# Weight split of a hybrid decoder layer: the gain moves from GpSimd into the ScalarE and VectorE splits, and the causal term of the first head from TensorE to VectorE

## What is computed

```python
def mixer_layer(x, conv_buf, c0, n0, m0, lead, norm_gain, w_in, ...):
    xn = rmsnorm(x, norm_gain)                       # x * rsqrt(mean x^2) * norm_gain
    proj = jnp.einsum('btd,dp->btp', xn, w_in)       # 1024 -> 9 * 512 + 8
    gb, gc, hc, zc, q, k, v, o, zm, ig, fg = jnp.split(proj, ...)
    yc, conv_new = short_conv(gc * hc, conv_buf, conv_w)
    y_conv = gb * yc * jax.nn.silu(zc)
    ...
    h = mlstm(q, k * HEAD_DIM ** -0.5, v, ig + b_igate, log_sigmoid(fg + b_fgate), state)
    ...                                              # per chunk of 128: exp(log_d - m), causal
    y_m = (rmsnorm(h) * mh_norm_gain * sigmoid(o)) * silu(zm)
    out = jnp.einsum('btw,wd->btd', concat([y_conv, y_m]), w_out)
    return x + out, ...
```

## Time and profile before

| | us |
|---|---|
| median of three runs | 1137.95 |
| lowest and highest run | 1137.59, 1143.83 |
| the profiled execution | 1141.33 |
| its span in the profile | 1139.5 |
| busy in the span: TensorE | 1071.2 (94%) |
| VectorE | 521.9 (46%) |
| ScalarE | 340.3 (30%) |
| GpSimd | 325.0 (29%) |
| mean granted TensorE clock | 0.985 |

### The profile page before, as it was taken

The page is one execution under the profiler, slowest core; times in us unless marked ns, Lnnn a source line. Parts: engine busy times, 40 slices in busy tenths (PEclk is TensorE's granted clock), DMA queues, the critical chain, the costliest instruction groups (busy, mean ns, idle before and its releaser), DMA issues. The chain is left out here.

```text
span 1139.5 us, 17968 instructions
## 1 busy us (share of the span) xinstructions
PE 1071.2 (94%) x7186; PEld 605.3 (53%) x7186; DVE 521.9 (46%) x981; ACT 340.3 (30%) x672; POOL 325.0 (29%) x370
## 2 busy tenths in 40 slices
PE   2799999998999999879999998899999999999996
PEld 2555546464666555536665655465656565444442
DVE  4886664555453434354433434544333233344333
ACT  6455534242412242322222223332222222221111
POOL 6432403043212323342122223431121111442322
PEclk9899999999999999999999999999999999999998
DMA  9464522043200311442002215310212044255652
GB/s 231 147 138 100 140 71 58 13 121 97 68 20 18 93 43 56 135 115 68 20 18 70 65 56 153 93 32 23 82 47 80 28 140 166 78 191 217 232 208 87
DMA packets 124184, 108.73 MB, mean 95 GB/s; under 512 B 42385, under 2 KB 109093, under 8 KB 124101
## 3 DMA queue, kind: packets, MB, share of 16 engines
q1 hardware_dynamic: 84160, 66.78, 20.1%
q0 software_dynamic: 7600, 25.03, 6.0%
q10 hardware_dynamic: 32340, 15.78, 5.2%
HBM read 65.43 MB, written 33.41 MB: 87 GB/s over the span
## 5 line engine op out<-in xcount | busy, mean ns | idle before, releaser
L824 PE MATMUL bank<-xTh,Wh 128*128 128x512 f16 (+2 forms) x1304 | 423.4, 344 | 7.9 <-DVE u L163 4.1
L825 PE MATMUL bank<-xTl,Wh 128*128 128x512 f16 (+2 forms) x1304 | 425.9, 344 | 0.0
L826 PE MATMUL bank<-xTh,Wl 128*128 128x512 f16 (+2 forms) x1304 | 425.0, 343 | 0.0
L826 PEld LDWEIGHTS bank<-xTh,Wl 128*128 128x128 f16 x1304 | 129.6, 99 | 122.0 <-issue 3.6
L824 PEld LDWEIGHTS bank<-xTh,Wh 128*128 128x128 f16 x1304 | 129.5, 99 | 117.9 <-DVE u L163 5.0
L825 PEld LDWEIGHTS bank<-xTl,Wh 128*128 128x128 f16 x1304 | 129.6, 99 | 109.8 <-issue 4.5
L833 PE MATMUL bank<-Wh,xTh 128*128 128x128 f16 x544 | 92.8, 219 | 1.4 <-DVE ysum L163 1.4
L835 PE MATMUL bank<-Wh,xTl 128*128 128x128 f16 x544 | 92.8, 219 | 0.0
L834 PE MATMUL bank<-Wl,xTh 128*128 128x128 f16 x544 | 92.8, 219 | 0.0
L610 POOL TENSOR_TENSOR wst<-wst,par 128x1024 f32<-128x1024 f32 x36 | 72.1, 2016 | 42.6 <-DMA wst<-in_w_in 42.3
L163 DVE SCALAR_TENSOR_TENSOR Wl<-wst,Wh 128x1024 f16<-128x1024 f32 x36 | 48.1, 1336 | 58.5 <-ACT Wh L163 56.3
(11 more groups left out here) (340 smaller groups left out, 1553.3 us busy)
## 6 DMA issues: line engine op xcount, KB each, us to landing
wst<-in_w_in ACTq DMA_DIRECT2D x27, 512.0 KB, 3.8
xs<-in_x_prompt SPq DMA_DIRECT2D x22, 512.0 KB, 4.0
y_ops<-ysumst POOLq DMA_DIRECT2D x16, 512.0 KB, 3.2
w_ops<-xs SPq DMA_DIRECT2D x16, 448.0 KB, 3.8
out<-xs POOLq DMA_DIRECT2D x11, 512.0 KB, 2.9
Wh<-y_ops SPq DMA_DIRECT2D x12, 448.0 KB, 3.6
Wl<-y_ops SPq DMA_DIRECT2D x12, 448.0 KB, 4.3
wst<-in_w_in SPq DMA_DIRECT2D x9, 512.0 KB, 4.9
```

The costliest lines, as they stand in the source:

```text
L824: mm(out, wh[:, k, :], xh, start=(k == 0), stop=False)
L825: mm(out, wh[:, k, :], xl, start=False, stop=False)
L826: last = mm(out, wl[:, k, :], xh, start=False, stop=(k == KT - 1))
```

## The change

GpSimd no longer multiplies weights by the gain. A new tile `wgain` holds 64 times the gain, and both splits take it as a scale for each partition. As the gain differs for each of the eight 128-row pieces k of a tile, each split is now eight instructions over 128 columns instead of one over 1024; each waits for the one before, and the other engine waits for the last. ScalarE's split waits for the load itself. In group 0 the two extra matmuls go, and the arguments are handled as in the other groups. The gate matmuls, the scan and the turn of blocks (0, 1) and (0, 2) come earlier. In the prologue the input parts of unit 3 come ahead of the gates' logits.

```diff
-GATES_AT = [ZC, HC, HC]
-SCAN_AT = [O, ZC, ZC]
-TURN_AT = [ZM, O, O]
+GATES_AT = [ZC, GC, GC]
+SCAN_AT = [O, GB, GB]
+TURN_AT = [ZM, ZC, ZC]
...
+        wgain = sb("wgain", [P, KT])
...
-            def gain_w(g, t):
-
-                pool.wait_ge(w_in_s[t % STAGES], g * (16 * NT // STAGES) + 16 * (t // STAGES + 1))
-                w = wst[t % STAGES]
-                pool.tensor_tensor(w[:, :, :], w[:, :, :], gain.unsqueeze(2).broadcast_to([P, KT, P]), ALU.mult).then_inc(w_gained, 1)
...
-                    if g:
-                        mm(A[:, :], selneg[:, :], m, start=True, stop=True).then_inc(a_full, 1)
-                    else:
-                        mm(A[:, :], selneg[:, :], m, start=True, stop=False)
-                        mm(A[:, :], identb[:, :], maskb[:, :].unsqueeze(1).broadcast_to([P, CH, P]), start=False, stop=True)\
-                            .then_inc(a_full, 1)
-                        pe.wait_ge(n_free, n)
-                        mm(N[0][:, :], selneg[:, :], m, start=True, stop=True).then_inc(e_full, 1)
+                    mm(A[:, :], selneg[:, :], m, start=True, stop=True).then_inc(a_full, 1)
...
-                act.wait_ge(w_gained, g * NT + (t + 1))
-                mark(fn(Wh[:, t, :, :], wst[t % STAGES][:, :, :], ACT.Copy, scale=WS).then_inc(w_high, 1), w_high, g * NT + (t + 1))
+                act.wait_ge(w_in_s[t % STAGES], g * (16 * NT // STAGES) + 16 * (t // STAGES + 1))
+                act.wait_ge(t1_free, 1)
+                for k in range(KT):
+                    last = fn(Wh[:, t, k, :], wst[t % STAGES][:, k, :], ACT.Copy, scale=wgain[:, k:k + 1])
+                    if k < KT - 1:
+                        did(last)
+                mark(last.then_inc(w_high, 1), w_high, g * NT + (t + 1))
...
             x_high_part(2)
             x_square(3)
+            x_high_part(3)
+            x_square(4)
             act.wait_ge(bias_in, 16 * 3)
             gate_logits(0, MIX, 1)
-            x_high_part(3)
-            x_square(4)
+            x_high_part(4)
             mixed_start(0, 0, K, True)
-            x_high_part(4)
...
                 dve.wait_ge(w_high, g * NT + (t + 1))
-                mark(stt(Wl[:, t, :, :], wst[t % STAGES][:, :, :], WS, Wh[:, t, :, :], ALU.mult, ALU.subtract).then_inc(w_low, 1), w_low, g * NT + (t + 1))
+                for k in range(KT):
+                    last = stt(Wl[:, t, k, :], wst[t % STAGES][:, k, :], wgain[:, k:k + 1], Wh[:, t, k, :], ALU.mult, ALU.subtract)
+                    if k < KT - 1:
+                        did(last)
+                mark(last.then_inc(w_low, 1), w_low, g * NT + (t + 1))
...
-                    if g:
-                        dve.wait_ge(a_full, n * 3 + 1)
-                        dve.wait_ge(y_sums, 4 * n)
-                        mark(tt(chunks(dp[:, :]), chunks(A[:, :]), maskb[:, :].unsqueeze(1).broadcast_to([P, CH, P]), ALU.add)
-                             .then_inc(arg_ready, 1), arg_ready, n + 1 - NB)
-                        dve.wait_ge(a_free, n * 3 + 1)
-                    else:
-                        dve.wait_ge(e_ready, n + 1)
+                    dve.wait_ge(a_full, n * 3 + 1)
+                    dve.wait_ge(y_sums, 4 * n)
+                    mark(tt(chunks(dp[:, :]), chunks(A[:, :]), maskb[:, :].unsqueeze(1).broadcast_to([P, CH, P]), ALU.add)
+                         .then_inc(arg_ready, 1), arg_ready, n + 1)
+                    dve.wait_ge(a_free, n * 3 + 1)
                     mark(tt(eh[:, :], eh[:, :], qf[:, :], ALU.mult).then_inc(q_scaled, 1), q_scaled, n + 1)
```

More of the change, by code:

```diff
@@ L295, in build @@
         xt_in = [sem(f"xt_in{i}") for i in range(3)]
-        w_gained, g_gained = sem("w_gained"), sem("g_gained")
+        g_gained, parts_clear = sem("g_gained"), sem("parts_clear")
         w_in_s = [sem(f"w_in{i}") for i in range(STAGES)]
@@ L304, in build @@
         a_full, a_free, s_full, s_free = sem("a_full"), sem("a_free"), sem("s_full"), sem("s_free")
-        e_full, e_ready, n_full, n_free = sem("e_full"), sem("e_ready"), sem("n_full"), sem("n_free")
+        n_full, n_free = sem("n_full"), sem("n_free")
         arg_ready, dp_ready = sem("arg_ready"), sem("dp_ready")
@@ L631, in _ @@
             x_power(4)
-            gain_w(0, 1)
-            gain_w(0, 2)
-            step(pool.memset(mparts[:, :], 0.0))
+            pool.memset(mparts[:, :], 0.0).then_inc(parts_clear, 1)
+            pool.wait_ge(parts_clear, 1)
             step(pool.memset(maskb[:, :], 0.0))
@@ L707, in store_mixed, with pool_block @@
                 pool.dma_start(dst, ystm[:, part, :, :]).then_inc(out, 16)
[L709 to L712, removed]
+            def pool_block(g, b, first):
                 for unit in ((), (11, 12), (15, 16))[b] if first else ():
                     x_power(unit)
-                weights(K, V)
                 if not (first and b == 0):
@@ L756, in _ @@
             for b in range(NB - 1):
-                pool_block(0, b, True, None)
+                pool_block(0, b, True)
             for g in range(1, H):
-                pool_block(g - 1, NB - 1, False, "weights")
+                pool_block(g - 1, NB - 1, False)
                 for b in range(NB - 1):
-                    pool_block(g, b, False, None)
-            pool_block(H - 1, NB - 1, False, None)
+                    pool_block(g, b, False)
+            pool_block(H - 1, NB - 1, False)
             store_y(H - 1, NB - 1, 1)
@@ L1253, in at_end @@
                     act.wait_ge(sel_ready, n + 1)
-                    if g:
-                        act.wait_ge(arg_ready, n + 1 - NB)
-                    else:
-                        act.wait_ge(ym_low, n)
-                        act.wait_ge(y_sums, 4 * n)
-                        act.wait_ge(a_full, n * 3 + 1)
-                    for out, src, kind, free, value in ((eh, A, 4, a_free, n * 3 + 1), (dp, dp, 3, dp_ready, n + 1 - NB)) if g else (
-                            (dp, A, 3, a_free, n * 3 + 1), (eh, N[0], 4, e_ready, n + 1)):
-                        if src is N[0]:
-                            act.wait_ge(e_full, n + 1)
+                    act.wait_ge(arg_ready, n + 1)
+                    for out, src, kind, free, value in ((eh, A, 4, a_free, n * 3 + 1), (dp, dp, 3, dp_ready, n + 1)):
                         for c in range(CH):
@@ L1649, in select @@
                 dve.wait_ge(tile_done, n * NT + 1)
-                if n <= NB:
-                    dve.wait_ge(e_ready, n)
-                else:
-                    dve.wait_ge(dp_ready, n - NB)
+                dve.wait_ge(dp_ready, n)
                 if b == 0:
@@ L1738, in at_end @@
                     if t == V:
+                        if b == 0:
+                            dve.wait_ge(parts_clear, 1)
                         gate_parts(tok0(b))
@@ L1818, in _ @@
             dve.wait_ge(t1_full, 1)
+            did(ts(wgain[:, :], T1[:, 0:KT], WS, None, ALU.mult))
             mark(copy(par[:, STATES_OUT:], T1[:, 0:PARAMS]).then_inc(t1_free, 1), t1_free, 1)
@@ L1826, in _ @@
             x_low_part(2)
+            x_low_part(3)
             dve.wait_ge(rows_const, 1)
```

17 lines of the change are left out of this document (1 added, 16 removed).

## The result

| | before | after |
|---|---|---|
| median of four runs, us | 1139.63 | 1178.97 |
| lowest and highest | 1137.59, 1143.83 | 1178.42, 1179.52 |
| span in the profile | 1139.5 | 1176.9 |
| busy: TensorE, VectorE, ScalarE, GpSimd | 1071.2, 521.9, 340.3, 325.0 | 1083.9, 563.1, 418.2, 246.1 |

The ratio is 1.034, with a 95% interval of 1.0307 to 1.0374: slower, where slower had been given 0.80. The time lies one us above the range. +25 us were predicted; the medians are 39.3 us apart, the two profiled executions and their spans 37.4.

What follows compares the result with a forecast made beforehand. TensorE, 94% busy, was taken to bound the kernel, with VectorE the engine making it wait. Terms 7.6 + 12 + 9.6 - 4.0 = +25 us gave 1163 us on the median; own range 1150 to 1174, whole range 1143 to 1178.

Steps and rivals of the forecast that it cites:

- The prices of a piece: Eight-piece splits: ScalarE piece 0.401 us, split 3.4 instead of 1.057; VectorE piece 0.349, split 3.05 instead of 1.23.
- Blocks (1,3) and (2,3): Same chain from a later load, new lateness partly replacing existing waits: 6 us each, together +12.
- Block (0,3): Step-by-step walk through both engines: the chunk waiting for update 0 comes 7.8 later; block loses 7.6 us.
- Block (0,0): Gates' rows 2.2 us earlier, mixed scores' product 8.9 later, then 2.9 more to the last state update: +9.6.
- The exponentials start about 2.0 later: Block (0,0), before the mixed scores' product: VectorE's mask addition stands behind a split and an input part, about 2.0 us.
- less about 3.1 of such waits: Block (0,0), last stretch: VectorE waits used up offset about 3.1 of O's 1.8 and ZM's 4.2, leaving +2.9.
- Blocks (0,1), (0,2): Scan moved -3.3, gate matmuls' wait in (0,1) +1.1, fewer matmuls in all four blocks -1.8: -4.0.
- the scan moves out: Scan leaves ZC in (0,1), ending TensorE's 1.67 us wait for the state, and one in the next block: -3.3.
- relief wins: First rival: GpSimd's relief outweighs splits if their pair in series takes 3.9 us, break-even 4.8; middle 1125 us, 8%.
- Late loads: Rival: ScalarE takes over GpSimd's load waits, showing at GB's split in three blocks, 3 x 3.7; 1174 us, 13%.
- Splits in between: Rival: pieces at 0.37 and 0.30, a pair of 5.3 us; 1144 us, 12%.
- no effect: Rival: splits cost nothing because they are off TensorE's path; 1132 us, 3%.

Runs made afterwards that it cites:

- e4: Changed kernel with pieces issued without waits between them and VectorE starting each piece when ScalarE's same piece is done; 1122.75 us, ratio 0.9841.
- e8: Changed kernel with no waits between pieces on either engine, VectorE still waiting for all eight of ScalarE's; 1138.81 us, ratio 0.9992.
- e5: Kernel before with only the first head's arguments changed: VectorE adds the mask, exponentials as in the other heads; 1143.51 us, ratio 1.0028.
- e6: Kernel before with only the three tables changed (places of gate matmuls, scan and turn); 1140.18 us, ratio 0.9997.
- e13: Changed kernel with throwaway matmuls filling TensorE's longest waits in blocks (0,3), (1,3), (2,3); 1179.67 us, ratio 1.0343.
- e1: Kernel before with only the eight-piece splits carrying the gain and GpSimd's multiplications gone; 1172.26 us, ratio 1.0274.
- e3: Changed kernel with both splits one 1024-column instruction with constant 64 and no multiplication by the gain anywhere; 1107.53 us, ratio 0.9709.
- e9: Changed kernel, waits between pieces kept, but VectorE starts each piece when ScalarE's same piece is done; 1162.84 us, ratio 1.0174.
- e11: Changed kernel with ScalarE's split one instruction with constant 64, VectorE's still eight pieces with the gain; 1151.44 us, ratio 1.0073.
- e15: Changed kernel with only ScalarE's eight pieces issued without waits between them; 1162.88 us, ratio 1.0196.
- e2: Changed kernel with GpSimd's gain and the long one-instruction splits kept, so only the rest of the change; 1144.42 us, ratio 1.0042.

## Why the prediction was right in kind and short in size

- **The prices of a piece** held: 0.401 on ScalarE, and 3.44 and 3.06 us a split. VectorE's form in PSUM was a good stand-in for SBUF. By the Trainium skill, "VectorE: DVE Perf Modes", section "The TRN2 errata", a split had been estimated at 2.3 and 1.6 us; without waits between pieces the rows show 2.44 and 2.19. The table is near ScalarE's independent instructions here, a quarter too low for VectorE's, and too low for chained ones on both. That the sum by the table would come near the first rival (1125) was not borne out: e4 (1122.75) is near it, but it also overlaps the engines; e8, without waits and in series as that rival has it, took 1138.81.
- **Blocks (1,3) and (2,3)**: +12 predicted, +13.1 measured. The walk through both engines' programs held for (1,3), and so did the argument that lateness replaces waits that were there. That the number fits so well is partly luck: (2,3) had been taken over from (1,3), and e5 and e6, which change nothing in these blocks, have (1,3) 2.4 and 1.7 and (2,3) 0.3 and 1.6 us shorter than the profile before, so each is known to about 2 us.
- **Block (0,3)**: +7.6 predicted, +11.4 measured. In the walk VectorE's split of V ends at 252.2. Counted from K's end (236.50 before, 249.33 after) it ended 1.1 us later: half is the steps between instructions, half GpSimd's additions beside it (3.60 instead of 3.06). `gcs` came 1.45 late, update 0 2.3 late, the last chunk 0.4 more, and a wait of 0.8 for `kfm` (the samples' keys, the first copy of the next block) stands behind ZM's split, where nothing had been counted. Small terms, all of one sign, are the error. The "two or three us" kept in hand for the clock were not it (e13). The walk had rightly put the exponentials behind the mask's addition and this behind the split of V: they start 18.5 us behind K's end, 17.2 in the walk, and 14.1 in e1, where TensorE adds the mask. This fits the 11.4 us that the block loses with both parts of the change, against 6.6 and 0.2 with each alone; a run of the splits with the arguments only was not made.
- **Block (0,0)**: +9.6 predicted, +12.55 measured. TensorE's start behind its waits for `drl`, `dpm` and `ysum`, before, after and in e1, cuts it into three stretches:

```profile
52.45 0.55 PE L859 MATMUL bank<-ident,arow 4*128 4x4 f32 x4 [6.58 <-DVE drl L163]
80.75 0.45 PE L975 MATMUL bank<-v1m,dpm 80*80 80x129 f32 x2 [0.94 <-DVE dpm L163]
114.64 0.23 PE L833 MATMUL bank<-Wh,xTh 128*128 128x128 f16 x1 [1.37 <-DVE ysum L163]
...
50.39 0.38 PE L839 MATMUL bank<-ident,arow 4*128 4x4 f32 x4 [3.98 <-DVE drl L163]
88.75 0.72 PE L948 MATMUL bank<-v1m,dpm 80*80 80x129 f32 x2 [2.58 <-DVE dpm L163]
127.19 0.23 PE L813 MATMUL bank<-Wh,xTh 128*128 128x128 f16 x1 [1.76 <-DVE ysum L163]
...
49.37 0.55 PE L848 MATMUL bank<-ident,arow 4*128 4x4 f32 x4 [3.74 <-DVE drl L163]
83.54 0.72 PE L964 MATMUL bank<-v1m,dpm 80*80 80x129 f32 x2 [3.91 <-DVE dpm L163]
121.99 0.23 PE L822 MATMUL bank<-Wh,xTh 128*128 128x128 f16 x1 [1.77 <-DVE ysum L163]
```

The stretches were predicted at -2.2, +8.9 and +2.9 and measured at -2.1, +10.1 and +4.55. Two steps failed. "The exponentials start about 2.0 later" is short: the new handling of the arguments adds 2.9 in the middle stretch and 4.45 in the whole block (e5). And in the last stretch "less about 3.1 of such waits" hid too much: O's and ZM's splits alone cost 4.6 there (e1), not 2.9. The splits' part as a whole, 7.6 in the working, measured 7.35 in e1, but as -3.1, +5.9 and +4.6 where -2.2, +6.9 and +2.9 had been worked out: errors that cancel, and so luck.
- **Blocks (0,1), (0,2)**, with the matmuls of all four blocks: -4.0 predicted, +0.3 measured in these two. The 1.8 for the matmuls held (e5), but 0.9 of it falls into (0,0) and (0,3), so for (0,1) and (0,2) it is -3.1 predicted. The gate matmuls' new wait, 1.1 in the working, is 1.27. In (0,2) the tables gave 1.9. In (0,1) they cost 3.0 (e6) instead of gaining half a us: "the scan moves out" was followed out of the old slot, not into the new one. This step has the wrong sign: -2.2 predicted for both blocks, +1.1 measured. The wait of 1.67 was to be gone from (0,1), and two others took its place; the lower clock that came with them, counted at nothing, made 1.9 of the 3.0.
- **The rivals**: "relief wins" was real as a term, 3% by e3, and lost to the pieces, but its rule, a pair of 4.8 us as the point from which it decides, fell with e9 to e11 and e15. "Late loads" fell with the 3.1 us that ScalarE waits for them in the changed kernel, and with e3. "Splits in between" and "no effect" fell with the pieces' rows and with e1.
- **The size**: with the matmuls' saving put where it falls, the misses are 3.4 in (0,0), 4.3 in (0,3), 1.1 in (1,3) and (2,3) and 3.4 in (0,1) and (0,2), in all the 12 us that are missing. The range allowed for the price of a split, which was right, and little for what a moved or added step does to its neighbours, which was wrong four times to the same side.

What stays open: how much of a us of a split is the engine's own time and how much the series, why a us of a split is worth more near the changed kernel than near e3, what TensorE's slow clock costs in (0,0), and the 1.2 us of e2 behind the `dpm` product.

## What to carry to other kernels

When an engine's long instruction becomes many short ones, price the waits between them too, and drop those that nothing needs: the same pieces made this kernel 3.4% slower with waits and 1.6% faster without them and overlapped. Read the price on each engine by itself: a us of VectorE, which holds the state's updates, was worth 2.3 times a us of ScalarE near e3 and 1.6 times near the changed kernel, and the length of their series alone ordered the runs wrongly. The series still counts: starting VectorE at ScalarE's first piece was worth 17 to 19 us here. A step that is moved must be walked into its new place on every engine, not only out of the old one.

## What was not expected of the hardware

- A wait on the own engine's previous piece costs 0.14 us on ScalarE (a step of 0.43, and 0.29 without it) and 0.13 on VectorE (0.387 and 0.26), with recorded durations nearly unchanged (0.401 and 0.386 for ScalarE). The records overlap when there is no wait.
- A second wait in front of each piece costs VectorE more: in e9 the step is (3.54 - 0.35) / 7 = 0.456, and 0.387 with one. It was 3.54 also for the split at 286.91, when ScalarE had finished with that tile at 285.2. In e4, where each piece waits for ScalarE alone and not for its own engine, such a wait costs nothing when ScalarE is already done: the split at 277.82 takes 2.19, a step of 0.26.
- Eight short VectorE pieces suffer from GpSimd too: 4.80 us for a split beside a GpSimd instruction of 2.2 us, 3.06 beside one of 0.40.
- TensorE's stretches at 1.2 GHz cost nothing in (0,3) of the changed kernel: 69.49 us with a granted clock of 0.93 and with 1.00. In (0,1), where TensorE sets the pace, the same 367 matmuls took 60.71 us at 0.97 (e6) and 58.82 at 1.00 (the kernel before).
